# Expert 0's token rows gathered in three groups, the last of them inside its first product; the starting terms of the output sums moved behind expert 1's first product; half of a weight chunk requested earlier

## The reference, cut to what matters

```
tok = rmsnorm(x)                                  # 256 x 1024
logits = tok @ router_w + router_b                # 32 experts
topv, topi = top_k(logits, 4); topw = softmax(topv)
combine = sum(one_hot(topi) * topw)               # 256 x 32
for e in range(32):
    gu   = tok @ w1[e] + b1[e]                    # w1[e]: 1024 x 2048
    gate = minimum(gu[:, :1024], 7); lin = clip(gu[:, 1024:], -7, 7)
    act  = (lin + 1) * gate * sigmoid(1.702 * gate)
    out += combine[:, e] * (act @ w2[e] + b2[e])  # w2[e]: 1024 x 1024
x = x + out
```

## Time and profile before

| | kernel before |
|---|---|
| median of three runs | 1113.23 us |
| lowest, highest | 1112.6, 1114.18 us |
| profiled execution, its own time | 1112.02 us |
| its span | 1110.3 us |
| TensorE busy | 1075.9 us, 97% |
| VectorE, ScalarE busy | 216.3 us, 160.8 us |
| HBM read | 431.15 MB |
| mean rate of the DMA over the span | 389 GB/s |

### The profile page before, as it was taken

One profiled execution on the slowest core, in us unless ns is written; L12 is line 12 of the kernel. 1 busy time (PEld: TensorE's weight loads), 2 busy tenths in 40 slices (PEclk: granted clock), 3 DMA queues, 4 the chain that ended last, 5 costly groups with the idle time before them and its releaser, 6 DMA issues.

```text
span 1110.3 us, 12071 instructions
## 1 busy us (share of the span) xinstructions
PE 1075.9 (97%) x5114; PEld 458.5 (41%) x5114; DVE 216.3 (19%) x521; ACT 160.8 (14%) x362; POOL 20.5 (2%) x38
## 2 busy tenths in 40 slices
PE   9999999999999999999999999999999999999997
PEld 6478885633333333333333333333233333333332
DVE  2722121321111111211111111111111111111111
ACT  2114201210000111111111111111011111111111
POOL 0006000000000000000000000000000000000000
PEclk9999999999999999999999999999999999999999
DMA  9924627999999999999999999999999999999996
GB/s 338 378 80 150 226 87 319 400 421 429 426 423 424 432 429 433 427 437 430 432 430 431 433 433 433 430 430 430 433 433 433 431 430 430 431 434 432 426 427 276
DMA packets 34891, 432.60 MB, mean 390 GB/s; under 512 B 3612, under 2 KB 5168, under 8 KB 17712
## 3 DMA queue, kind: packets, MB, share of 16 engines
q1 hardware_dynamic: 32672, 430.73, 92.1%
q10 hardware_dynamic: 2192, 1.48, 0.5%
HBM read 431.15 MB, written 1.05 MB: 389 GB/s over the span
## 4 chain that ended last, share of the span: by engine, by line
PE 64%; DMA 33%; DVE 2%; issue 0%; ACT 0%; SPq 0%
DMA ring<-in_expert_w_dram 32%; PE bank L399 24%; PE bank L428 14%; PE bank L1330 5%; PE bank L437 4%; PE bank L1394 2%; PE bank L362 2%; PE bank L1404 2%; PE bank L389 2%; PE bank L1253 2%; PE bank L1314 1%; PE bank L376 1%; PE bank L411 1%; PE bank L381 1%; PE bank L1226 1%; DVE ring L967 1%
## 5 line engine op out<-in xcount | busy, mean ns | idle before, releaser
L399 PE MATMUL bank<-ring,work 128*64 128x512 f32 x2048 | 451.5, 596 | 15.6 <-DMA ring<-in_expert_w_dram 15.6
L399 PEld LDWEIGHTS bank<-ring,work 128*64 128x64 f32 x2048 | 143.3, 137 | 320.8 <-issue 289.6
L428 PE MATMUL bank<-ring,work 128*64 128x512 f32 x992 | 219.4, 593 | 11.4 <-DMA ring<-in_expert_w_dram 11.3
L428 PEld LDWEIGHTS bank<-ring,work 128*64 128x64 f32 x992 | 74.9, 137 | 151.2 <-issue 148.9
L1104 DVE TENSOR_SCALAR work<-bank 128x512 f32<-128x512 f32 x31 | 21.4, 692 | 459.8 <-PE bank L399 459.8
L826 ACT ACTIVATE work<-work 128x512 f32<-128x512 f32 x31 | 19.5, 630 | 497.7 <-DVE work L1104 497.7
L463 DVE TENSOR_TENSOR work<-bank,vecs 128x512 f32<-128x512 f32 x31 | 21.4, 691 | 209.9 <-PE bank L376 209.9
L437 PE MATMUL bank<-work,putT 64*128 64x512 f32 x248 | 61.9, 616 | 0.0
L362 PE MATMUL bank<-xs,pick 128*64 128x512 f32 x248 | 58.5, 592 | 0.0
L1330 PE MATMUL bank<-ring 128*128 128x256 f32 x256 | 56.6, 380 | 0.0
L1330 PEld LDWEIGHTS bank<-ring 128*128 128x128 f32 x256 | 48.2, 190 | 6.7 <-issue 0.3
(11 more groups left out here) (210 smaller groups left out, 523.7 us busy)
## 6 DMA issues: line engine op xcount, KB each, us to landing
ring<-in_expert_w_dram SPq DMA_DIRECT2D x70, 4096.0 KB, 39.5
ring<-in_expert_w_dram SPq DMA_DIRECT2D x39, 2048.0 KB, 15.9
ring<-in_expert_w_dram SPq DMA_DIRECT2D x21, 1024.0 KB, 10.5
ring<-in_w_in_dram SPq DMA_DIRECT2D x8, 2048.0 KB, 21.0
ring<-in_w_out_dram SPq DMA_DIRECT2D x2, 2048.0 KB, 8.1
ring<-in_w_branch_attn_dram SPq DMA_DIRECT2D x1, 2048.0 KB, 7.9
ring<-in_w_branch_pool_dram SPq DMA_DIRECT2D x1, 2048.0 KB, 8.9
work<-in_expert_w_dram SPq DMA_DIRECT2D x2, 1024.0 KB, 13.7
```

What stands on the lines that cost most here:

```text
L399: mm = pe.matmul(dst, hTe[:, at:at + SLOTS], w[a][:, col:col + BANK], start=(k == 0 and not bias_first), stop=(k == KD - 1 and bias_first) ...
L428: mm = pe.matmul(ps[SLOTS * half:SLOTS * (half + 1), :], actT[:, at:at + SLOTS], w[a // 2][:, col:col + BANK], start=(k == 0), stop=(k == ...
```

## The change

Four things are edited; the sums and products computed stay the same.

1. `gather_first` works on three groups of blocks, 0 and 1, 2 and 3, 4 to 7, in three banks. Groups 0 and 1 are gathered before `up_first`. Of group 2 two blocks of the first token half are gathered there too; the rest of it and `count_tokens` stand inside chunk 1 of `up_first`. Chunks 0 and 1 wait for groups 0 and 1, chunk 2 for group 2. VectorE moves `weigh(0)` and `weigh(1)` between the copies of groups 1 and 2.
2. `transpose_weight` and `start_acc` move from between expert 0's and expert 1's first products to the step behind expert 1's first product, on either side of `gather_expert(2)`. ScalarE's copy of the weights moves behind `actT_out(0)`.
3. The first half of `w2` of expert 0, second chunk, is requested behind chunk 2 of expert 0's `w1`, not behind `load_w2(0, 0)`.
4. The semaphore `half_ok` of VectorE's `glu` is merged into `lin_ok`, and a semaphore `weight_ps` is new.

```diff
-        first_ps = (ps_gather, bank[3])
+        first_ps = (ps_gather, bank[3], bank[1])
+        FIRST = (range(0, 2), range(2, 4), range(4, 8))
...
-        def gather_first(pe, tt, half, blocks=range(4)):
-            for j in blocks:
-                mm = pe.matmul(first_ps[half][:, j * SLOTS:(j + 1) * SLOTS], every(xs[:, tt, :], W1_ROWS, 4 * half + j), pick[:, tt, :],
+        def gather_first(pe, tt, group, blocks=range(4)):
+            for j, k in list(enumerate(FIRST[group]))[blocks.start:blocks.stop]:
+                mm = pe.matmul(first_ps[group][:, j * SLOTS:(j + 1) * SLOTS], every(xs[:, tt, :], W1_ROWS, k), pick[:, tt, :],
...
             load_w1(0, 2)
+            n, src = w2_chunk(0, 1), w2_dram(0, 1)
+            sp.dma_start(chunk_halves(n)[0], src[:, 0:CHUNK_N // 2]).then_inc(chunk_in[EXTRA], 16)
             used(B_WP)
             load_w1(0, 3)
...
             load_w2(0, 0)
-            n, src = w2_chunk(0, 1), w2_dram(0, 1)
-            sp.dma_start(chunk_halves(n)[0], src[:, 0:CHUNK_N // 2]).then_inc(chunk_in[EXTRA], 16)
             used(B_WO + 1)
...
             sigmoid_gate(0)
-            act.wait_ge(put_ps, 1)
-            nc.scalar.copy(weightT, ps_out[:, T:2 * T]).then_inc(s["weightT_sb"], 1)
             putT_out(0)
             rows_out(1)
             actT_out(0, False)
+            act.wait_ge(s["weight_ps"], 1)
+            nc.scalar.copy(weightT, ps_out[:, T:2 * T]).then_inc(s["weightT_sb"], 1)
...
-            weigh(0)
...
-                dve.wait_ge(lin_ok, e + 1)
+                dve.wait_ge(lin_ok, 2 * e + 1)
...
-                                               op1=ALU.mult).then_inc(half_ok, 1)
-                dve.wait_ge(half_ok, e + 1)
+                                               op1=ALU.mult).then_inc(lin_ok, 1)
+                dve.wait_ge(lin_ok, 2 * e + 2)
...
-            for half, (ready, done) in enumerate(((first_gathered, first_hT), (rowsT_ps, hTe_ok))):
-                dve.wait_ge(ready, 1)
-                gain = ...
-                nc.vector.tensor_tensor(...).then_inc(done, 1)
+            def first_rows_in(group):
+                at, n = FIRST[group].start, len(FIRST[group])
+                half, j = at // 4, at % 4
+                gain = vecs[:, V_G2 + at:V_G2 + at + n].rearrange("p (j a) -> p j a", a=1).to_broadcast([P, n, SLOTS])
+                return nc.vector.tensor_tensor(hTe.rearrange("p (j h n) -> p j h n", j=4, h=2)[:, j:j + n, half, :],
+                                               first_ps[group][:, 0:n * SLOTS].rearrange("p (j n) -> p j n", j=n), gain, ALU.mult)
+            for group in range(2):
+                dve.wait_ge(first_gathered, group + 1)
+                first_rows_in(group).then_inc(first_hT, 1)
+            weigh(0)
+            weigh(1)
+            dve.wait_ge(rowsT_ps, 1)
+            first_rows_in(2).then_inc(hTe_ok, 1)
             build_pick(slot_id, 1).then_inc(pick_ok, 1)
...
-            weigh(1)
...
-            gather_first(pe, 0, 0, range(0, 2))
+            gather_first(pe, 0, 0)
             place_tokens(1)
-            gather_first(pe, 0, 0, range(2, 4))
             gather_first(pe, 0, 1)
+            gather_first(pe, 0, 2, range(0, 2))
             pe.wait_ge(s["first_pick"], 2)
             gather_first(pe, 1, 0).then_inc(first_gathered, 1)
-            gather_first(pe, 1, 1).then_inc(rowsT_ps, 1)
-            count_tokens()
+            gather_first(pe, 1, 1).then_inc(first_gathered, 1)
...
             def up_first():
-                pe.wait_ge(first_hT, 1)
                 for c in range(W1_CHUNKS):
...
-                    if c == 2:
+                    if c < 2:
+                        pe.wait_ge(first_hT, c + 1)
+                    elif c == 2:
                         pe.wait_ge(hTe_ok, 1)
-                    mm = up_early(w, c)
+                    if c == 1:
+                        gather_first(pe, 0, 2, range(2, 4))
+                        up(pe, w, c, range(0, 1)).then_inc(half_used, 1)
+                        gather_first(pe, 1, 2).then_inc(rowsT_ps, 1)
+                        count_tokens()
+                        mm = up(pe, w, c, range(1, W1_ROWS))
+                    else:
+                        mm = up_early(w, c)
...
             up_first()
-            transpose_weight()
             transpose_put_expert(0)
             gather_expert(1)
-            start_acc()
...
                 up_expert(i, j + 1, up_chunk)
+                if first:
+                    transpose_weight()
                 gather_expert(e + 2)
+                if first:
+                    start_acc()
                 down_expert(i, j, down_chunk)
```

More of the change, by code:

```diff
@@ L199, in block_kernel @@
             pooled_ps pooled_sb branch_ps merge_ok out_ps x1_ok x1_rms
-            x1T_ps x1T_act x1T_dve rw_ok groups_ps groups_sb logits2_ps rt_top rt_exp rt_ok weight_ok weightT_sb first_pick place_ps
+            x1T_ps x1T_act x1T_dve rw_ok groups_ps groups_sb logits2_ps rt_top rt_exp rt_ok weight_ps weight_ok weightT_sb first_pick place_ps
             most_ok result_dve result_act stored bias_ok""".split()
@@ L203, in block_kernel @@
         dve_step, act_step, pool_step = sem("dve_step"), sem("act_step"), sem("pool_step")
-        pick_ok, gathered, hTe_ok, gemm1, gate_ok, sig_ok, half_ok, glu_ok = (
-            sem(n) for n in "pick_ok gathered hTe_ok gemm1 gate_ok sig_ok half_ok glu_ok".split())
+        pick_ok, gathered, hTe_ok, gemm1, gate_ok, sig_ok, glu_ok = (
+            sem(n) for n in "pick_ok gathered hTe_ok gemm1 gate_ok sig_ok glu_ok".split())
         put_ok, put_ps, put_sb, actT_ps, actT_sb, gemm2, out_ok, lin_ok, rows_ok, rowsT_ps = (
@@ L1125, in glu_last @@
                     dve.wait_ge(gate_ok, E + h)
-                    dve.wait_ge(lin_ok, E + h)
+                    dve.wait_ge(lin_ok, 2 * E - 1 + h)
                     nc.vector.scalar_tensor_tensor(out=pairs(lin_e, h), in0=pairs(lin_e, h), scalar=1.0, in1=pairs(gate_e, h),
-                                                   op0=ALU.add, op1=ALU.mult).then_inc(half_ok, 1)
-                    dve.wait_ge(half_ok, E + h)
+                                                   op0=ALU.add, op1=ALU.mult).then_inc(lin_ok, 1)
+                    dve.wait_ge(lin_ok, 2 * E + 1 + h)
                     dve.wait_ge(sig_ok, E + h)
@@ L1132, in glu_last @@
                                             ALU.mult).then_inc(glu_ok, 1)
-            for half, (ready, done) in enumerate(((first_gathered, first_hT), (rowsT_ps, hTe_ok))):
-                dve.wait_ge(ready, 1)
-                gain = vecs[:, V_G2 + 4 * half:V_G2 + 4 * half + 4].rearrange("p (j a) -> p j a", a=1).to_broadcast([P, 4, SLOTS])
-                nc.vector.tensor_tensor(hTe.rearrange("p (j h n) -> p j h n", j=4, h=2)[:, :, half, :],
-                                        first_ps[half][:, 0:4 * SLOTS].rearrange("p (j n) -> p j n", j=4), gain, ALU.mult).then_inc(done, 1)
+            def first_rows_in(group):
[11 more added lines that the diff above has]
+            first_rows_in(2).then_inc(hTe_ok, 1)
             build_pick(slot_id, 1).then_inc(pick_ok, 1)
@@ L1449, in transpose_weight @@
                 for tt in range(TT):
-                    pe.transpose(ps_out[:, T + tt * P:T + (tt + 1) * P], weight[:, tt, :], ident[:, :])
+                    mm = pe.transpose(ps_out[:, T + tt * P:T + (tt + 1) * P], weight[:, tt, :], ident[:, :])
+                mm.then_inc(s["weight_ps"], 1)
             def add_x1(j):
@@ L1603, in _, with step @@
             up_first()
-            transpose_weight()
             transpose_put_expert(0)
             gather_expert(1)
-            start_acc()
             transpose_act_expert(0, False)
             transpose_rows_expert(1, False)
-            def step(i, j, up_chunk, down_chunk, act_wide, rows_wide):
+            def step(i, j, up_chunk, down_chunk, act_wide, rows_wide, first=False):
                 e = i * TURN + j
                 up_expert(i, j + 1, up_chunk)
+                if first:
+                    transpose_weight()
                 gather_expert(e + 2)
+                if first:
+                    start_acc()
                 down_expert(i, j, down_chunk)
@@ L1623, in _ @@
             for j in range(TURN):
-                step(0, j, up_early, down_early, j + 1 >= W2_WIDE, j + 2 >= W1_WIDE)
+                step(0, j, up_early, down_early, j + 1 >= W2_WIDE, j + 2 >= W1_WIDE, j == 0)
                 if j in (1, 2):
```

## The result

| | before | changed |
|---|---|---|
| median | 1113.21 us (21 runs, 1111.47 to 1114.46) | 1114.00 us (21 runs, 1113.15 to 1115.9) |
| ratio to before | | 1.0012, 95% interval 1.0006 to 1.0017 |
| span of the profiled execution | 1110.3 us | 1111.9 us |

The ratio, taken over all runs, is 1.3 us (0.7 to 1.9). The two medians are 0.8 us apart and the two means 1.3 us, so the size of the loss is known to about half a microsecond; its sign is clear. The predicted 1112.6 and the range up to 1113.9 both missed the 1114.00.

The account below looks back on a forecast made before the run. The weight stream at 430 GB/s was taken as the bound, unbroken from R20 on. R20 landing 0.4 to 0.6 us earlier, 0.6 taken, gave 1113.2 - 0.6 = 1112.6 us; range 1110.9 to 1113.9.

Parts of the forecast that it names:

- R20: Weight request for a whole chunk, released by use of expert 2's first chunk; forecast to land at 270.8, 0.4 us earlier.
- part 2: Gather in three groups: up(0) starts 1.6 us earlier and ends as before; four switches inside chunk 1 taken as 0.
- part 3: Sums' first terms moved behind expert 1's first product: that product starts 0.6 us earlier, everything from expert 0's second 0.8 later.
- R9: First half-chunk request of the second group of eight; forecast to land at 238.3, 0.8 us earlier.
- F: What a request meeting an idle stream pays on top of its bytes; taken as about 4.1 us, other end 2.8.
- up(0): First product of expert 0; forecast to start at 208.74, 1.6 us earlier, and end at 224.24 as before.
- R1: Request released by use of expert 0's first half chunk; forecast issued at 210.65, landing 217.35, 1.6 us earlier.
- R8: Last of the first group of eight half-chunk requests; forecast to land at 234.8, 1.6 us earlier.
- Part 1: Half chunk requested earlier, in the idle stretch: takes 2.44 us from the later queue, later landing 0.7 to 2.1 us earlier.
- rival (d): The moved half chunk does nothing, only the other two parts gain: same 1112.6; chance 0.58 together with the forecast.
- rival (c): Switches in chunk 1 cost 1.0 us in all; R20 issued at 262.7, landing 0.6 us later: 1113.8; chance 0.12.
- Theory B: From the experiments, not the prediction: at the late first 4 MiB request earlier stream losses vanish; only TensorE's lateness there counts.

Follow-up runs that it names:

- the additions late: Changed kernel with TensorE's two additions of x to the sums moved behind the steps of experts 3 and 4: ratio 1.0007 (0.9998 to 1.0016) to before.
- The kernel with all the cures: Changed kernel with group 2's rest and count in one piece ahead of chunk 1's product, additions of x late, first 4 MiB requests in two: 1.0007 to before.

## Why the prediction was wrong

**The view of what bounds the kernel** was right: the stream does, and the rate from 600 to 1055 us is 431 GB/s in both traces.

**Two steps failed, one behind the other.** The first is the sum up to R20, "R20 at the later of 270.4 and 261.7 + 9.1 = 270.8, 0.4 earlier than 271.2". R20 went out at 262.73 and landed at 272.9 (272.7 to 273.3 in four traces), 1.7 us later than before in the two first traces. Its terms were too small: TensorE's switches, put at 0, cost 0.70 us in part 2 and some 0.3 in part 3, and R9's F was 5.4 in place of 4.2. The prediction had named the sign of this: wrong "if up(0) ends more than 0.4 us later". It ended 0.70 later.

The second is "From R20 on the stream is unbroken and the gain is kept to the end", with the slack that "grows from there". I had looked at one request behind R20, at 288.64, and reasoned on from the mean lengths of a step and of its bytes. The slack was gone at 316.43, and the first 4 MiB request at 326.89 falls short by 1 us before the change. So TensorE's lateness ahead of it counts: 3.4 us of it cost 2.4, 1.7 us cost 1.0, and 1.9 us with the change 1.3 (with the half chunk late, and the stream at R20 as before, 1.6). Behind it 3.4 us cost 0.9, with an interval from 0 to 1.9. So the gains at R1 to R8 would most likely have been lost here even if R9 and R20 had kept them: the run with the half chunk late has its stream at R20 1.4 us or more ahead of the changed kernel's, and is no faster.

**Part 1** was right: no gain (0.9997), as rival (d) had it. It wasn't seen that R9's hole would be deeper with the half early (7.8 us in place of 5.8).

**Part 2**: start of up(0) and R1 right to 0.1 us. The term "four of them, 0 to 0.2 us each; I take 0" was mis-sized: 0.70 us in all. This was rival (c)'s mechanism, given 0.12. Its R20 at 262.7 came out exactly, in part by luck: it has 1.0 us from part 2 alone, and measured were 0.70 there and some 0.3 in part 3.

**Part 3**: up(1) 0.54 earlier (0.6 predicted), up(2) 1.20 later in the run with this part alone, 0.8 predicted; again switches, 0.15 twice. I had counted it as covered by R20's slack.

**A reading of the page** was loose: the DMA share is 9 in every slice from the eighth on but the last, which has 6. Nothing hangs on it.

**F**: "I take F about 4.1" treated one request's latency as a constant. R1 alone shows 3.0 or less to 5.2, R9 of the changed kernel 5.4, and R9 with the gather alone 2.5, the lowest of the requests by halves in any trace. The Trainium skill's 2.0 us (DMA: Bandwidth & Descriptors, "Anatomy of one DMA"), fitted for transfers that GpSimd issues, was not reached.

**What stays open.** Theory B in its strict form, that only TensorE's lateness at that request reaches the end, isn't shown; two sets of runs speak against it. First, making TensorE earlier at the request, or the request independent of it, gave the kernel before nothing (0.9996, 0.9999, 1.0002), where 1 us was expected. Second, the same cures on the kernels with all three parts leave 1.0007 each time (the request in two, the additions late, and both), some 0.8 us, where theory B expected from 0 to 0.6. Single intervals are too wide for either, but three runs agree in each set. A reading that fits most of it, and that no run isolates, is that two things make the changed kernel late by about as much at this point: the request's issue (1.9 us) and the stream's own landings, from R9 and R20 on (the last one before the request comes at 331.9 to 332.6 in the four traces, at 329.9 to 330.7 in those with the requests of before up to R20, leaving out the run with 3.4 us of work ahead). Then taking away one of the two, as the run with the half late and the run with the request in two do, leaves most of the loss. The kernel with all the cures doesn't fit it: in its trace that landing is at 330.6.

Every trace has a few single losses of 1 to 2 us between 200 and 490 us, at changing places, and behind 490 only one in all traces is over 1 us (1.5 us at 1079, in the second trace of the changed kernel). While few requests wait, such a loss reaches the end unless a later shortage hides it; that would explain why curing one shortage buys nothing, but no run here isolates it either.

## What to carry to other kernels

Where a stream of transfers sets the end, find the last request that is issued too late for it, by going through issue and landing of every request until the queue holds several; what is gained ahead of it can be lost there, and what makes it later is paid. A change in the form of the requests (two chunks in one) is the first place to look at, since it waits for the later of two places. And in a chain that has no pause, count each passage between matmuls whose stationary operands differ in width. Where the forecast effect is under 0.1% of the time, as here, a landing read in one trace (good to about 1 us) can't carry it: take times from many runs, and from traces only what repeats in several.

## What had not been expected of the hardware

- TensorE pays some 0.3 us each time it goes from the product (stationary 128x64) to expert 0's gather (stationary 128x128) and back, about 0.15 on either piece, though its weight loads are idle two thirds of the time. Between the later gather and the product, both with a stationary operand of 128x64, it pays nothing (1.72 us for L362, 1.87 behind a transpose).
- The latency of a request that meets a dry stream scatters by 2 us between executions of one program (5.4, 6.7, 7.6 us for R1, where the stream itself allowed no less than the 5.4), while the issue times repeat to 0.01 us.
- With one request taken out of a busy stretch, a later hole was deeper: R9 lands 5.8 us after its issue with the half late (one trace; 4.9 in that of the gather alone) and 7.5 to 7.9 with it early (four), with R8 landing at 235.3 in the first and at 234.9 to 235.3 in the four. The cause isn't shown, and the kernel with all the cures, which has the half early too, lands R9 after 6.4 us.
